# A hybrid decoder step on one core: the low weight halves of eight more phases come from adding transfers

## The chip, the cores and the metric

The kernel runs on one core of one Trainium2 chip. Its metric is the device time of one execution, in microseconds (us), given as the median of several runs; less is better. A core has a matrix engine (TensorE, in the rows PE for its matmuls and PEld for its weight loads), a vector engine (VectorE, DVE), an activation engine (ScalarE, ACT), a general engine (GpSimd, POOL) and a sequencer that mostly issues transfers (SyncE, SP). Each engine runs its own list of instructions in order; semaphores tie the lists together. Transfers are issued by SP or by GpSimd and run on 16 shared DMA engines.

## The reference

One layer of a decoder for 512 prompt tokens and 8 x 4 sample tokens (544 columns in all), in float32. The weight matrices are what is streamed; cut to them, the layer is:

```python
h = rmsnorm(x, norm1_g)
a1, a2, z, xbc, dt_raw, u, v = split(h @ w_in)
y_a = silu(layernorm(causal_dwconv(a1 * sigmoid(a2)))) @ conf_w_out
y_ssd = ssd(silu(causal_dwconv(xbc)), softplus(dt_raw + bias), ...)   # 16 heads, state 128
y_b = rmsnorm((y_ssd + D * xs) * silu(z), ssm_norm_g) @ ssm_w_out
y_c = (gelu(u) * chunk_spatial(layernorm(gelu(v)))) @ gmlp_w_out
gates = sigmoid(h @ w_gate + b_gate)                                  # three gates
x = x + (gates[0] * y_a + gates[1] * y_b + gates[2] * y_c) @ w_o
up = rmsnorm(x, norm2_g) @ ffn_w_up                                   # 2 x 2816 wide
x = x + (silu(causal_dwconv(up[..., :2816])) * up[..., 2816:]) @ ffn_w_down
```

The new states of the three convolutions, of the recurrence and the normalised v are outputs too, and y is the final rmsnorm of x.

## The kernel before

**Arithmetic.** TensorE multiplies in a rounded float32 (fp32r). For accuracy every weight and every activation is kept as a high part, which is the value rounded to fp32r, and a low part, which is the value less its high part. A product is made of three matmuls: high by high, high by low and low by high. The tokens lie in two halves of 272 columns, so one block of 128 weight rows (a k-block) costs 6 matmuls: a slot of 8 k-blocks 48, one of 6 k-blocks 36, one of 5 k-blocks 30.

**Slots, quads and phases.** `w_split[:, s, 0]` and `w_split[:, s, 1]` hold the high and low part of slot s, `w_raw[:, s]` the float32 weights as loaded. There are four slots; one filling of all four is a quad. The work is twelve phases one after the other, with their quads and the k-blocks of a slot: A (2 quads), VU (2), X (3), G2 (4), G0 (4), Z (2), G1 (4), WO (2), U1 (6), all of 8 k-blocks, where G2 and G0 have 4 in every second slot, then D1 (4 quads of 6 k-blocks), U2 (5 of 8) and D2 (4 of 5). In D1 and D2, the two parts of the last projection, two slots in a row (a pair) add up to one output block; elsewhere each slot is an output block of its own.

**The life of a slot.** SP loads the raw weights (`load_quad`, L329). When TensorE has finished the block that used the slot (`acc_full`), ACT evacuates it, then makes the slot's new parts from `w_raw` (`split_hi`, L348, called in `act_quad`, L377). In D1 and D2 the evacuation point comes once in a pair, so both slots of a pair are refilled after the pair. The low half is made in one of two ways. In the quads from the second of A to the first of Z ("added" quads, `is_added`), ACT writes the negative of the rounded weights into the low half (L352) and the high half after it (L353), and GpSimd issues a transfer that adds the raw weights from memory onto the low half (`add_raw`, L361). From the second quad of Z to the end, ACT writes only the high half, and GpSimd subtracts it from the raw weights (`split_lo`, L355, the instruction on L358). TensorE waits for the low half of a slot before the slot's first matmul (`wait_lo` in `pe_quad`, L403). In the last quad of D2 (`last_halves`, L1421) TensorE takes the first token half over all four slots and then the second half, so it comes to the second pair of slots after 30 matmuls rather than 60.

**Who waits for whom.** After its loads, SP waits for the low half of the quad before (subtracted quads) or for the high half (added quads) until it overwrites `w_raw`. GpSimd's list is in program order: `pool_phase` (L598) gives per pair the phase's own work (in the up projections the convolution's edges, L620 to L627) and then the low halves of the quad ahead. Two of its phases hold the last slot of the quad ahead until a value is ready ("hold"), and in Z (L664 to L673) the last slot of G1's first quad waits for `ssm_lo`, the split of the recurrence's output, whose room it takes. In G1 the activations come from that split, made by VectorE (L2023) out of a long chain on `xbc` (L1945, L1957, L1988).

Of the kernel before, what the change touches and what calls it, by code (L numbers as in the profile page):

```python
# [20 lines left out]
ALU = mybir.AluOpType  # L21
# [67 lines left out]
def phases():  # L89
    out, q, p = {}, 0, 0  # L90
    for name, quads, kb, per_block in PHASES:
        out[name] = Phase(name, quads, kb, per_block, q, p)
        q += quads
        p += quads * (2 // per_block)
    return out
# [19 lines left out]
def loop(e, lo, hi, body):  # L115

    if hi - lo == 1:
        body(lo)
    elif hi > lo:
        with e.Fori(lo, hi) as i:  # L120
            body(i)


def wait(e, sem, value):

    if isinstance(value, int) and value <= 0:
        return
    e.wait_ge(sem, value)
# [11 lines left out]
def build(nc, ins, outs):  # L140
    ph = phases()
    order = [x[0] for x in PHASES]
    with ExitStack() as ctx:
        def sb(name, shape, dt=F32):
            return ctx.enter_context(nc.sbuf_tensor(name, shape, dt))
# [10 lines left out]
        w_split = sb("w_split", [P, SLOTS, 2, ELEM], F32R)  # L156
# [131 lines left out]
        w_hi = [sem(f"w_hi{s}") for s in range(SLOTS)]  # L288
        w_lo = [sem(f"w_lo{s}") for s in range(SLOTS)]
        w_added = [sem(f"w_added{s}") for s in range(SLOTS)]  # L290
# [20 lines left out]
                return ins["ffn_w_up"], i * 4 + ((0 if name == "U1" else 2 * FFA) + s)  # L311
            return ins["ffn_w_down1" if name == "D1" else "ffn_w_down2"], i * 4 + s

        added_first, added_end = ph["A"].quad0 + 1, ph["Z"].quad0 + 1

        def is_added(p, i):
            return isinstance(i, int) and added_first <= p.quad0 + i < added_end

        def wait_lo(e, p, i, s, back=0):

            q = p.quad0 - back
            if isinstance(i, int) and added_first <= q + i < added_end:
                e.wait_ge(w_added[s], 16 * (q + i + 1 - added_first))
            elif isinstance(i, int) and q + i < added_first:
                wait(e, w_lo[s], q + i + 1)
            else:
                e.wait_ge(w_lo[s], i + (q + 1 - (added_end - added_first)))

        def load_quad(sp, p, i):  # L329
            for s in range(SLOTS):  # L330
                src, j = w_src(p.name, i, s)
                n = p.kb[s] * P
                if isinstance(i, int) and added_first < p.quad0 + i <= added_end:
                    sp.wait_ge(w_hi[s], i + p.quad0)
                elif not isinstance(i, int) or p.quad0 + i > 0:
                    wait_lo(sp, p, i, s, 1)
                ap = src[j] if isinstance(j, int) else src[bass.ds(j, 1)].rearrange("o p n -> (o p) n")
                sp.dma_start(w_raw[:, s, 0:n], ap).then_inc(w_landed[s], 16)

        def load_phase(sp, name, first=0):  # L340
            p = ph[name]
            if p.quad0 <= added_end:
                for i in range(first, p.quads):
                    load_quad(sp, p, i)
            else:
                loop(sp, first, p.quads, lambda i: load_quad(sp, p, i))

        def split_hi(act, p, i, s):  # L348
            n = p.kb[s] * P
# [5 lines left out]
        def split_lo(e, p, i, s):  # L355
            n = p.kb[s] * P
            e.wait_ge(w_hi[s], i + (p.quad0 + 1))
            e.tensor_tensor(w_split[:, s, 1, 0:n], w_raw[:, s, 0:n], w_split[:, s, 0, 0:n].bitcast(F32),  # L358
                               ALU.subtract).then_inc(w_lo[s], 1)

        def add_raw(pool, p, i, s):  # L361

            src, j = w_src(p.name, i, s)
            n = p.kb[s] * P
            pool.wait_ge(w_hi[s], p.quad0 + i + 1)
            pool.dma_start(w_split[:, s, 1, 0:n], src[j], accum_op=ALU.add).then_inc(w_added[s], 16)  # L366

        def head_groups():

# [227 lines left out]
        def _(pool):  # L597
            def pool_phase(name, work, hold=None):  # L598


                p = ph[name]

                def quad(i, ahead, hold=None):
                    for r in range(2):
                        work(i, r)
                        if ahead is not None:
                            split_lo(pool, ahead[0], ahead[1], 2 * r)
                            if hold is not None and r == 1:
                                pool.wait_ge(sem(hold), KD)
                            split_lo(pool, ahead[0], ahead[1], 2 * r + 1)  # L610
                loop(pool, 0, p.quads - 1, lambda i: quad(i, (p, i + 1)))
                quad(p.quads - 1, after(p), hold)

            def nothing(i, r):
# [49 lines left out]
            p = ph["Z"]  # L664
            for i in range(p.quads):
                for s in range(SLOTS):
                    q, j = (p, i + 1) if i + 1 < p.quads else after(p)
                    if (i, s) == (1, 0):
                        for n in range(STATES_Z):
                            decay_state(n)  # L670
                    if (i, s) == (1, 3):
                        pool.wait_ge(sem("ssm_lo"), KD)
                    split_lo(pool, q, j, s)  # L673
            pool_phase("G1", nothing, "mx_lo")
            pool_phase("WO", nothing, "n2_lo")
            pool.wait_ge(sem("merged"), 16)
# [1677 lines left out]
```

## Time and profile before

| what | value |
|---|---|
| runs | 1003.36, 1005.99, 1001.53 us; median 1003.36 us |
| the profiled execution | 1004.03 us; its span 1001.8 us; mean granted clock 0.996 |
| busy in the span | PE 984.0 us (98%), DVE 607.3 (61%), ACT 437.6 (44%), POOL 310.8 (31%) |
| transfers issued by GpSimd | 60 adding transfers, 27.27 MB, the queue's packets 15.5% of 16 engines |
| transfers issued by SP | 97.09 MB, 32.1% |

The profiled execution is 0.67 us above the median of the runs. A time in the rows below is counted from the start of the span. TensorE is busy nearly all the time, so what other engines do matters only where TensorE has to wait for it; the chain of waits and the timelines show such places as a number in square brackets, the idle time before a row and what ended it.

### The profile page before, as it was taken

The numbers are of one execution on the slowest core, as the hardware profiler recorded it, in microseconds if no ns is written. First come the engines' busy times: TensorE is split into PE (matmuls) and PEld (weight loads), VectorE is DVE, ScalarE is ACT, GpSimd is POOL, SyncE is SP. The second block draws the span as 40 slices with busy tenths as digits, with TensorE's granted clock in tenths as the row PEclk, the third lists the DMA queues.
The fourth block names the chain that finished last, engine by engine and source line by source line (L and its number), as shares of the span: only waits on it lengthen the run. The fifth ranks groups of instructions, "written<-read, shape, count | busy, mean of one in ns | idle before, by whom it ended". The sixth has DMA issues, their size and how long they took to land.

```text
span 1001.8 us, 19136 instructions
## 1 busy us (share of the span) xinstructions
PE 984.0 (98%) x7849; PEld 963.6 (96%) x7849; DVE 607.3 (61%) x955; ACT 437.6 (44%) x619; POOL 310.8 (31%) x261
## 2 busy tenths in 40 slices
PE   8899999999999999999999999999999999999997
PEld 8799999999998999899999999999999999999997
DVE  7599799962645675797744247555540036565456
ACT  7554579575734775525233344444321132232120
POOL 0111111111111114344342444444433464444341
PEclk9899999999999999999999999999999999999999
DMA  7888769667765768315272223222223332321222
GB/s 227 251 184 181 164 144 151 143 128 169 160 149 125 181 143 223 110 64 168 85 257 84 85 85 105 85 84 84 63 63 95 115 106 86 93 79 52 70 71 90
DMA packets 52590, 125.24 MB, mean 125 GB/s; under 512 B 15920, under 2 KB 18864, under 8 KB 52528
## 3 DMA queue, kind: packets, MB, share of 16 engines
q1 hardware_dynamic: 43744, 97.09, 32.1%
q0 software_dynamic: 8640, 27.27, 15.5%
q8 instruction: 45, 0.74, 0.3%
q14 instruction: 17, 0.14, 0.1%
q10 hardware_dynamic: 144, 0.00, 0.0%
HBM read 116.41 MB, written 7.93 MB: 124 GB/s over the span
## 4 chain that ended last, share of the span: by engine, by line
PE 90%; DVE 3%; DMA 2%; SPq 2%; ACT 1%; issue 1%; DVEq 0%; ACTq 0%
PE accs L418 82%; PE accs L1438 2%; DMA w_split<-in_w_in_main 1%; DMA w_split<-in_w_gate 1%; PE misc L1213 1%; SPq L513 1%; DVE part L494 1%; PE misc L1178 1%; DMA w_raw<-in_w_in_main 1%; PE misc L1037 1%; PE misc L1218 1%; PE misc L1197 1%; DVE xbc L1945 0%; PE misc L1163 0%; PE misc L1229 0%
## 5 line engine op out<-in xcount | busy, mean ns | idle before, releaser
L418 PE MATMUL accs<-h_split,w_split 128*128 128x272 f32 x4608 | 584.4, 288 | 0.1
L418 PEld LDWEIGHTS accs<-h_split,w_split 128*128 128x128 f32 x4608 | 576.9, 188 | 5.6 <-issue 4.4
L418 PE MATMUL accs<-branch,w_split 128*128 128x272 f32 x2472 | 320.5, 290 | 7.0 <-DMA w_split<-in_w_in_main 5.0
L418 PEld LDWEIGHTS accs<-branch,w_split 128*128 128x128 f32 x2472 | 314.3, 189 | 11.7 <-DMA w_split<-in_w_in_main 5.2
L358 POOL TENSOR_TENSOR w_split<-w_raw,w_split 128x1024 fp32r<-128x1024 f32 (+2 forms) x104 | 234.7, 2264 | 209.5 <-ACT w_split L353 186.0
L353 ACT ACTIVATE w_split<-w_raw 128x1024 fp32r<-128x1024 f32 (+3 forms) x166 | 157.8, 959 | 202.0 <-PE accs L418 201.8
L1522 DVE SCALAR_TENSOR_TENSOR ca<-part,params,ca 128x512 f32<-128x512 f32 x120 | 82.5, 744 | 0.1
L366 POOL DMA_DIRECT2D w_split<-in_w_in_main x24 | 21.1, 879 | 153.7 <-ACT w_split L353 153.7
L2202 DVE TENSOR_TENSOR xbc<-accs,xbc 128x544 f32<-128x544 f32 x14 | 10.1, 725 | 87.7 <-PE accs L418 87.7
L352 ACT ACTIVATE w_split<-w_raw 128x1024 fp32r<-128x1024 f32 (+1 forms) x60 | 56.1, 936 | 15.9 <-PE accs L418 12.7
L2179 DVE TENSOR_TENSOR temps<-temps,mixed 128x512 f32<-128x512 f32 x22 | 40.7, 1850 | 26.5 <-ACT temps L1011 26.5
L865 ACT ACTIVATE temps<-accs,params 128x544 f32<-128x544 f32 x24 | 17.2, 715 | 81.3 <-PE accs L418 81.2
L366 POOL DMA_DIRECT2D w_split<-in_w_gate x16 | 13.9, 870 | 109.8 <-ACT w_split L353 109.8
L2164 DVE TENSOR_TENSOR temps<-accs,mixed 128x272 f32<-128x272 f32 (+2 forms) x66 | 18.8, 340 | 44.0 <-PE accs L418 43.9
L2175 DVE SCALAR_TENSOR_TENSOR temps<-temps,params 128x560 f32<-128x560 f32 x44 | 37.4, 850 | 6.1 <-DVE temps L2172 1.5
L2191 DVE TENSOR_TENSOR branch<-temps,branch 128x544 f32 (+1 forms) x22 | 25.9, 1178 | 22.2 <-ACT branch L1016 22.2
L1011 ACT ACTIVATE temps<-temps,params 128x560 f32<-128x560 f32 x22 | 16.8, 764 | 47.4 <-DVE temps L2175 47.3
L1621 DVE SCALAR_TENSOR_TENSOR temps<-temps,params 128x568 f32<-128x568 f32 x36 | 29.0, 807 | 5.8 <-ACT temps L815 5.6
L2090 DVE TENSOR_TENSOR temps<-accs,temps 128x544 f32<-128x544 f32 x8 | 5.8, 725 | 37.5 <-PE accs L418 37.5
L626 POOL COPY tail_f<-temps 128x2 f32 (+1 forms) x22 | 4.5, 205 | 75.7 <-DVE temps L2164 75.7
L2144 DVE TENSOR_TENSOR xbc<-accs,xbc 128x544 f32<-128x544 f32 x8 | 5.8, 725 | 31.2 <-PE accs L418 31.2
L1908 DVE TENSOR_SCALAR temps<-misc,small 128x128 f32<-128x128 f32 x64 | 17.3, 342 | 10.6 <-PE misc L1197 10.6
(280 smaller groups left out, 793.4 us busy)
## 6 DMA issues: line engine op xcount, KB each, us to landing
w_raw<-in_ffn_w_up SPq DMA_DIRECT2D x44, 512.0 KB, 3.6
w_raw<-in_w_in_main SPq DMA_DIRECT2D x28, 512.0 KB, 4.6
w_split<-in_w_in_main POOLq DMA_DIRECT2D x24, 512.0 KB, 8.0
w_raw<-in_w_gate SPq DMA_DIRECT2D x24, 512.0 KB, 3.9
w_split<-in_w_gate POOLq DMA_DIRECT2D x16, 512.0 KB, 7.9
w_raw<-in_ffn_w_down SPq DMA_DIRECT2D x16, 384.0 KB, 3.1
w_raw<-in_ffn_w_down SPq DMA_DIRECT2D x16, 320.0 KB, 2.9
xbc<-in_x SPq DMA_DIRECT2D x16, 272.0 KB, 5.8
```

Of the source, the lines that this page charges most:

```text
L352: act.activation(w_split[:, s, 1, 0:n], w_raw[:, s, 0:n], ACT.Copy, scale=-1.0)
L353: act.activation(w_split[:, s, 0, 0:n], w_raw[:, s, 0:n], ACT.Copy).then_inc(w_hi[s], 1)
L358: e.tensor_tensor(w_split[:, s, 1, 0:n], w_raw[:, s, 0:n], w_split[:, s, 0, 0:n].bitcast(F32), ALU.subtract).then_inc(w_lo[s], 1)
L366: pool.dma_start(w_split[:, s, 1, 0:n], src[j], accum_op=ALU.add).then_inc(w_added[s], 16)
L418: mm = pe.matmul(accs[:, a, half, 0:HALF], w_split[:, s, wp, k * P:(k + 1) * P], rhs(s, k, xp, half), start=(first and k == 0 and n == 0), ...
L1438: mm = pe.matmul(accs[:, a, half, 0:HALF], w_split[:, s, wp, k * P:(k + 1) * P], rhs(s, k, xp, half), start=(s % 2 == 0 and k == 0 and n = ...
L1522: ins_ = dve.scalar_tensor_tensor(out=dst, in0=src, scalar=w, in1=dst, op0=ALU.mult, op1=ALU.add)
L1621: dve.scalar_tensor_tensor(out=cv, in0=src, scalar=w, in1=cv, op0=ALU.mult, op1=ALU.add)\
L2164: ins_ = dve.tensor_tensor(dst, src, st, ALU.mult)
L2175: dve.scalar_tensor_tensor(out=cv, in0=src, scalar=w, in1=cv, op0=ALU.mult, op1=ALU.add)\
L2179: dve.tensor_tensor(sil, sil, stat_n2[:, 0:SEQ], ALU.mult)
L2191: dve.tensor_tensor(pick(branch, i * 2 + (12 + r)), prod, pick(branch, i * 2 + r).bitcast(F32), ALU.subtract).then_inc(sem("f_lo"), 1)
```

## The change

All quads but the first of A become added ones: `is_added` holds from A's second quad to the end, also where the quad is a loop's register. ACT makes two copies for every slot, GpSimd issues an adding transfer where it subtracted, TensorE waits for that transfer's semaphore (`w_added`) and SP for ACT's (`w_hi`). `pool_phase` is written out quad by quad instead of a hardware loop, and SP's loads always run in a loop. The subtracting instructions of GpSimd that go are 72 of 128x1024, 16 of 128x768 and 16 of 128x640, and as many adding transfers come in their place. Line numbers of the changed kernel are 4 to 6 lower from L353 on.

```diff
-        added_first, added_end = ph["A"].quad0 + 1, ph["Z"].quad0 + 1
+        added_first = ph["A"].quad0 + 1
 
         def is_added(p, i):
-            return isinstance(i, int) and added_first <= p.quad0 + i < added_end
+            return not isinstance(i, int) or p.quad0 + i >= added_first
 
         def wait_lo(e, p, i, s, back=0):
 
             q = p.quad0 - back
-            if isinstance(i, int) and added_first <= q + i < added_end:
-                e.wait_ge(w_added[s], 16 * (q + i + 1 - added_first))
-            elif isinstance(i, int) and q + i < added_first:
+            if isinstance(i, int) and q + i < added_first:
                 wait(e, w_lo[s], q + i + 1)
             else:
-                e.wait_ge(w_lo[s], i + (q + 1 - (added_end - added_first)))
+                e.wait_ge(w_added[s], i * 16 + 16 * (q + 1 - added_first))
 
         def load_quad(sp, p, i):
...
-                if isinstance(i, int) and added_first < p.quad0 + i <= added_end:
+                if not isinstance(i, int) or p.quad0 + i > added_first:
                     sp.wait_ge(w_hi[s], i + p.quad0)
-                elif not isinstance(i, int) or p.quad0 + i > 0:
+                elif p.quad0 + i > 0:
                     wait_lo(sp, p, i, s, 1)
...
         def load_phase(sp, name, first=0):
             p = ph[name]
-            if p.quad0 <= added_end:
-                for i in range(first, p.quads):
-                    load_quad(sp, p, i)
-            else:
-                loop(sp, first, p.quads, lambda i: load_quad(sp, p, i))
+            loop(sp, first, p.quads, lambda i: load_quad(sp, p, i))
...
-            pool.wait_ge(w_hi[s], p.quad0 + i + 1)
-            pool.dma_start(w_split[:, s, 1, 0:n], src[j], accum_op=ALU.add).then_inc(w_added[s], 16)
+            pool.wait_ge(w_hi[s], i + (p.quad0 + 1))
+            ap = src[j] if isinstance(j, int) else src[bass.ds(j, 1)].rearrange("o p n -> (o p) n")
+            pool.dma_start(w_split[:, s, 1, 0:n], ap, accum_op=ALU.add).then_inc(w_added[s], 16)
...
                         if ahead is not None:
-                            split_lo(pool, ahead[0], ahead[1], 2 * r)
+                            add_raw(pool, ahead[0], ahead[1], 2 * r)
                             if hold is not None and r == 1:
                                 pool.wait_ge(sem(hold), KD)
-                            split_lo(pool, ahead[0], ahead[1], 2 * r + 1)
-                loop(pool, 0, p.quads - 1, lambda i: quad(i, (p, i + 1)))
+                            add_raw(pool, ahead[0], ahead[1], 2 * r + 1)
+                for i in range(p.quads - 1):
+                    quad(i, (p, i + 1))
...
                     if (i, s) == (1, 3):
                         pool.wait_ge(sem("ssm_lo"), KD)
-                    split_lo(pool, q, j, s)
+                    add_raw(pool, q, j, s)
```

GpSimd's list in D2, the last phase, before: a loop over the quads, where each row names the line, the instruction, what it writes and reads, and in brackets the semaphores it waits for.

```order
L120 UNCONDITIONAL_BRANCH
L120 ISA
L358 TENSOR_TENSOR w_split<-w_raw,w_split 128x640 [waits w_hi0]
L358 TENSOR_TENSOR w_split<-w_raw,w_split 128x640 [waits w_hi1]
L358 TENSOR_TENSOR w_split<-w_raw,w_split 128x640 [waits w_hi2]
L358 TENSOR_TENSOR w_split<-w_raw,w_split 128x640 [waits w_hi3]
L120 REGISTER_ALU
L120 COMPARE_AND_BRANCH
```

The same place after: the last two quads written out, each row a transfer from `ffn_w_down`.

```order
L361 DMA w_split<-in_ffn_w_down 128x640 [waits w_hi0]
L361 DMA w_split<-in_ffn_w_down 128x640 [waits w_hi1]
L361 DMA w_split<-in_ffn_w_down 128x640 [waits w_hi2]
L361 DMA w_split<-in_ffn_w_down 128x640 [waits w_hi3]
L361 DMA w_split<-in_ffn_w_down 128x640 [waits w_hi0]
L361 DMA w_split<-in_ffn_w_down 128x640 [waits w_hi1]
L361 DMA w_split<-in_ffn_w_down 128x640 [waits w_hi2]
L361 DMA w_split<-in_ffn_w_down 128x640 [waits w_hi3]
```

The waits are the same ones in the same order; the subtraction became a transfer's issue, and the semaphore that TensorE waits for is now counted up by the transfer's landing.

GpSimd's list at the end of Z, before: the low halves of Z's second quad, GpSimd's share of the state update (L494), and those of G1's first quad.

```order
L358 TENSOR_TENSOR w_split<-w_raw,w_split 128x1024 [waits w_hi3]
L494 TENSOR_TENSOR part<-part,small 128x512 [waits s_off,s_last]
L494 TENSOR_TENSOR part<-part,small 128x512 x3
L358 TENSOR_TENSOR w_split<-w_raw,w_split 128x1024 [waits w_hi0]
L358 TENSOR_TENSOR w_split<-w_raw,w_split 128x1024 [waits w_hi1]
L358 TENSOR_TENSOR w_split<-w_raw,w_split 128x1024 [waits w_hi2]
L358 TENSOR_TENSOR w_split<-w_raw,w_split 128x1024 [waits w_hi3,ssm_lo]
```

And after, with the same values under line numbers 5 lower.

```order
L361 DMA w_split<-in_w_in_z 128x1024 [waits w_hi3]
L489 ISA
L489 TENSOR_TENSOR part<-part,small 128x512 [waits s_off,s_last]
L489 TENSOR_TENSOR part<-part,small 128x512 x3
L361 DMA w_split<-in_w_gate 128x1024 [waits w_hi0]
L361 DMA w_split<-in_ssm_w_out 128x1024 [waits w_hi1]
L361 DMA w_split<-in_w_gate 128x1024 [waits w_hi2]
L361 DMA w_split<-in_ssm_w_out 128x1024 [waits w_hi3,ssm_lo]
```

The state update stays GpSimd's and stays at its place; before and behind it stand transfers' issues, and the last of them still waits for `ssm_lo`.

## Rows read from the trace of the kernel before

**Rows 1.** The page, first part: busy us (share of the span) x instructions.

```profile
PE 984.0 (98%) x7849; PEld 963.6 (96%) x7849; DVE 607.3 (61%) x955; ACT 437.6 (44%) x619; POOL 310.8 (31%) x261
```

**Rows 2.** The chain that ended last: start us, us, what.

```profile
599.83 375.61 PE accs L418 x3012
975.45 9.41 PE accs L1438 x75
```

**Rows 3.** Stretches: length, busy PE PEld DVE ACT POOL, clock, DMA, GB/s.

```profile
34.40:37.00 2.60, 0.00 (x0) 0.00 (x0) 1.78 (x4) 1.71 (x3) 0.00 (x0) 1.00 1.01 233
37.00:44.00 7.00, 4.62 (x20) 4.62 (x21) 5.25 (x10) 4.92 (x7) 1.83 (x2) 0.51 0.97 241
40.00:101.00 61.00, 61.00 (x476) 61.00 (x476) 54.64 (x89) 27.34 (x34) 8.89 (x11) 0.97 0.83 189
450.00:460.00 10.00, 8.39 (x63) 7.88 (x62) 7.88 (x13) 6.82 (x10) 1.74 (x1) 1.00 0.60 211
930.00:975.00 45.00, 45.00 (x361) 45.00 (x361) 20.30 (x20) 8.24 (x12) 20.37 (x11) 1.00 0.25 71
```

**Rows 4.** PE in time order, [idle before <-releaser]: 20:70 and 425:470.

```profile
39.38 26.36 PE L418 MATMUL accs<-branch,w_split 128*128 128x272 f32 x192 [4.99 <-DMA w_split<-in_w_in_main]
...
430.60 0.94 PE L1364 MATMUL misc<-branch 96*128 96x512 f32 x3
...
437.35 1.46 PE L1364 MATMUL misc<-branch 96*128 96x512 f32 x3
...
455.86 2.70 PE L418 MATMUL accs<-branch,w_split 128*128 128x272 f32 x18 [1.60 <-DVE branch L2023]
...
466.05 4.17 PE L418 MATMUL accs<-branch,w_split 128*128 128x272 f32 x32
```

**Rows 5.** DVE in order of time, 425 to 460 us.

```profile
431.87 2.88 DVE L1945 TENSOR_TENSOR xbc<-xbc,temps 128x512 f32<-128x512 f32 x1
...
443.42 0.69 DVE L1945 TENSOR_TENSOR xbc<-xbc,temps 128x512 f32<-128x512 f32 x1
```

**Rows 6.** POOL in order of time, 423 to 470 us.

```profile
428.58 5.62 POOL L358 TENSOR_TENSOR w_split<-w_raw,w_split 128x1024 fp32r<-128x1024 f32 x2
...
458.26 4.74 POOL L358 TENSOR_TENSOR w_split<-w_raw,w_split 128x1024 fp32r<-128x1024 f32 x2 [16.68 <-DVE branch L2023]
```

**Rows 7.** Line L366, the adding transfers: issue ns, landing us; then windows 185:204, 229:232.

```profile
L366 POOL DMA_DIRECT2D w_split<-in_w_in_main x24: 853/868/1016, 30.2 to 175.6; - x24
...
DMA to landing us min/median/max: 4.4/7.8/12.6
...
DMA to landing us min/median/max: 4.4/4.7/8.1
...
DMA to landing us min/median/max: 8.5/8.6/8.7
```

**Rows 8.** POOL's and ACT's groups by form: busy us, mean ns, idle before.

```profile
L358 POOL TENSOR_TENSOR w_split<-w_raw,w_split 128x1024 fp32r<-128x1024 f32 x72 | 176.3, 2451 | 140.9 <-ACT w_split L353 117.3 <-DVE branch L2023 16.7 <-DVE branch L2106 6.8
...
L353 ACT ACTIVATE w_split<-w_raw 128x1024 fp32r<-128x1024 f32 x118 | 123.9, 1052 | 102.2 <-PE accs L418 102.0
```

**Rows 9.** PE in order of time, 735 to 1002 us.

```profile
738.56 72.32 PE L418 MATMUL accs<-branch,w_split 128*128 128x272 f32 x576
...
930.19 45.26 PE L418 MATMUL accs<-branch,w_split 128*128 128x272 f32 x360
975.29 9.57 PE L1438 MATMUL accs<-branch,w_split 128*128 128x272 f32 x75
```

**Rows 10.** ACT in order of time, in D1 and D2.

```profile
747.87 1.58 ACT L353 ACTIVATE w_split<-w_raw 128x768 fp32r<-128x768 f32 x2 [7.31 <-PE accs L418]
...
937.99 1.37 ACT L353 ACTIVATE w_split<-w_raw 128x640 fp32r<-128x640 f32 x2 [5.70 <-PE accs L418]
...
975.48 1.37 ACT L353 ACTIVATE w_split<-w_raw 128x640 fp32r<-128x640 f32 x2 [6.06 <-PE accs L418]
```

**Rows 11.** POOL in order of time, D2's end.

```profile
976.30 3.58 POOL L358 TENSOR_TENSOR w_split<-w_raw,w_split 128x640 fp32r<-128x640 f32 x2 [3.35 <-ACT w_split L353]
```

## The prediction

> **What bounds the kernel now.** I read the engines' busy time first: TensorE works 984.0 of 1001.8 us [rows 1], so all its idle time is 17.8 us and no change to the other engines can gain more than that. The chain of waits says where it is: from 599.83 us on, the chain is 3012 matmuls without a break for 375.61 us, then the last quad [rows 2]; one matmul is 375.61 / 3012 = 0.1247 us. So from the first up projection to the last quad nothing is to be gained, and everything that comes late is paid in full. What can be gained lies before, and of it the change touches only the end of Z, where the timeline of TensorE shows two stalls on VectorE: 1.60 us before 455.86, and three small products that take 1.46 us where their like take 0.94, about 0.5 us [rows 4]. The rows on the adding transfers give the new operation's price: 0.86 us of GpSimd to issue one, and 4.4 to 12.6 us until it has landed, 7.8 in the middle [rows 7]. A subtraction takes 2.45 us for 128x1024 [rows 8] and 1.8 for 128x640 (two in 3.58) [rows 11]. The low half of a slot thus comes some 4 to 6 us later than now wherever GpSimd is not backed up, and the question at each slot is whether TensorE is then still busy with the others.
>
> **Where the delay is hidden.** With one block a slot, a refilled slot is needed again after the three other slots, 3 x 48 x 0.1247 = 18.0 us. Evacuation and two copies take some 4 us, a landing 7.8, so 6 us remain in U1, U2, WO and G1, and I cost these at nothing; without that cover each landing above 14 us would be paid. ACT's second copy, 72 x 1.05 us and 32 of 0.7 to 0.8, brings it from 438 to about 537 us of 1002 [rows 1, 8]: hidden, as ACT's wait for TensorE before these copies is 102 us. SP gets its go from ACT's high half instead of from GpSimd, so raw loads start earlier; they were landed in time already: nothing. GpSimd's unrolled list: nothing, since it is busy 31% [rows 1] and loses 235 us of subtractions for 104 x 0.87 = 90 us of issues. The extra traffic is 104 adds, about 47 MB over the last 550 us; the DMA engines are 0.25 busy there now [rows 3].
>
> **The end of Z (a gain).** The first VectorE row at 431.87 takes 2.88 us while GpSimd subtracts from 428.58 on, and its like at 443.42, with GpSimd at rest, 0.69 [rows 5, 6]. VectorE has no pause from there to the split that ends the 1.60 us stall. Without the subtractions the chain comes 2.2 us earlier, which covers 1.60 and 0.5: -2.1. Bounds: -2.1 (nothing else is there to gain) and 0 (if the issues of transfers hold VectorE up the same way). Against it stands the hold on slot 3 of G1's first quad: what GpSimd waited 16.68 us for came at 458.26 [rows 6]; 2.2 earlier is 456.06, and with a landing of 7.8 it is there at 463.9. TensorE starts on that slot at 466.05 [rows 4], 2.1 earlier 463.95. That is level, so I add 0.3 for scatter; a landing of 12.6 would cost 4.7.
>
> **Into U2 (a loss).** In D1 both slots of a pair are refilled after the pair and needed again after one other pair. A pair of D1 takes 72.32 / 8 = 9.04 us [rows 9]. ACT starts 0.27 us after the end of it (747.87 less 738.56 and 9.04) [rows 9, 10]; two copies of U2's 512 KB slot take 2.10 [rows 8]; GpSimd starts 0.13 after a copy (976.30 less 975.48 and one copy of 0.69) [rows 10, 11]. Left for the landing: 9.04 - 0.27 - 2.10 - 0.13 = 6.5 us. Two adds close together landed after 8.5 to 8.7 us (the last line of [rows 7]); I take 8.6: late by +2.1, once, at U2's first slot. Bounds 0 and 6.1 (a landing of 12.6).
>
> **Within D1.** The same with copies of 1.58: 7.06 us are left for 384 KB. The stretch with two 256 KB adds and one of 512 KB, each alone, has 4.4, 4.7 and 8.1 [rows 7]; on a line from 4.4 to 8.1, 384 KB take 6.25, and a partner cost 8.7 - 8.1 = 0.6: 6.85. Just in time; +0.2 for scatter, bounds 0 and 4.6 (three late pairs at 8.6).
>
> **Within D2.** A pair takes 45.26 / 6 = 7.54 us [rows 9], ACT starts 0.26 after it and makes two copies in 1.37 [rows 10]: 7.54 - 0.26 - 1.37 - 0.13 = 5.78 us are left. By the same line 320 KB take 5.3, with a partner 5.9: late by 0.1. A late pair gives the next one as much more room, so only the first pair of each of three quads pays: +0.3. In the last quad the second pair is needed after 30 matmuls, 3.74 us. ACT starts at 975.48, 0.19 after the pair before has ended [rows 9, 10], so 3.74 - 0.19 - 1.37 - 0.13 = 2.05 us are left where a subtraction needs 1.8 today. It is late by 5.9 - 2.05 - 0.1 = +3.75. D2 together +4.1; bounds +2.3 (the least landing of the trace, 4.4) and +12 (8.6 for every pair).
>
> **The clock.** After the one long wait on an add, 4.99 us, the next 192 matmuls took 26.36 us instead of 23.94 [rows 4]; the granted clock was 0.51 (1.2 of 2.4 GHz) from 37 to 44 us after 1.00 before it. After the 1.60 us stall it stayed at 1.00 [rows 3]. The 3.75 us wait in the last quad lies nearer to the first: +2.4, bounds 0 and 2.4.
>
> **Sum.** -2.1 + 0.3 + 2.1 + 0.2 + 4.1 + 2.4 = +7.0, that is 1011.0 for the profiled execution of 1004.03, which lies 0.67 above the median; on the median of 1003.36 it is 1010.4.
>
> A rule that would change the sum: the Trainium skill, "DMA: Bandwidth & Descriptors", section "Anatomy of one DMA — SWDGE (gpsimd) path", fits a transfer issued by GpSimd as 2.0 us plus its bytes over 436 GB/s, by which 320 KB would be an estimated 2.75 us and 512 KB 3.2. Only the last quad would then be late, by 0.7, and the sum would be -1.1, 1002.3. The trace disagrees for the adding form: none of 60 landed in under 4.4 us [rows 7]; what the rule would do is part of rival (3) below.
>
> **Rivals.** (1) All as above, but the clock holds through the 3.75 us wait: +4.6, 1008.0. For it: the only drop in the rows came after 5 us with the DMA full. (2) The adds land quicker where little else is moved: in D2 the DMA engines are 0.25 busy against 0.83 from 40 to 101 us, in the stretch of the earlier adds [rows 3]. With 5.1 us for 320 KB (midway from 4.4 to 5.9) and 7.8 for the 512 KB pair: D2 +3.05, U2 +1.3, gain -2.1, sum +2.2, 1005.6; with the clock's drop 1008.0. (3) Not slower: adds so quick that only the last quad waits. From 4.1 us for 320 KB on down, and 6.5 for 512 KB, its wait is paid by the gain at Z; at 4.4, the least of the 60, the sum is +0.3, 1003.7. Against it: that least one moved 256 KB. (4) GpSimd's issues suffer from VectorE, so that an add takes 8.6 us even in D2: three pairs late by 2.8, the last one by 3.75, D1 +4.6, U2 +2.1, clock +2.4, gain -2.1: +19.2, 1022.6. Against it: issues took 853 to 1016 ns over the whole trace, where VectorE was busy 54.64 of 61 us too, and the middle landing was 7.8 [rows 3, 7]. The skill's "SBUF — State Buffer", section "SBUF: two separate sides", warns of just this, that some VectorE instructions keep GpSimd from writing a transfer's descriptors; that busy stretch does not bear it out. (5) VectorE is not freed, or slot 3 of G1 is caught by its hold: the gain is lost and up to 1.7 us come on top, +9 to +11, 1012.4 to 1014.
>
> **How the numbers follow.** The case of the sum 0.42, (1) 0.15, (2) 0.20, (3) 0.06, (4) 0.06, (5) 0.11. A measurement of this kernel tells 0.5%, 5.0 us, from no change; the border is 1008.4. The case of the sum lies 2 us above it and counts 0.85 slower (0.36); (1) lies on it, 0.45 (0.07); (2) 0.25 (0.05); (4) all (0.06); (5) 0.8 (0.09): slower 0.63. Faster than 998.3 needs more than the 2.1 us I can find: 0.04. Same: 0.33. The likeliest's own range is 1007 to 1014; the range takes in (2) down to 1004.5 and (5) and half of the way to (4) up to 1016. Predicted: 1010.4.
>
> **What the profile of the changed kernel would show.** The adds of 320 KB with their landing times: 5.3 to 6.5 us bears the D2 step out, under 4.5 kills it. TensorE's timeline: a wait on the add of `ffn_w_down` of 3 to 4.5 us within the last quad, one of 1 to 3 us at U2's first slot, almost none inside U1, U2, WO and G1, and no 1.6 us stall on VectorE at the end of Z. The granted clock behind the last wait: 0.5, or 1.0 for rival (1). VectorE's row at the place of 431.87 at 0.7 instead of 2.88. Waits above 2 us at every pair of D2 would be rival (4). The prediction is wrong if waits show up in the one-block phases, where I count on 6 us of room.

## The result and the profile after

The changed kernel takes 1010.73 us (median of 7 runs, 1008.74 to 1012.23) against 1003.51 us (7 runs, 1001.53 to 1005.99): ratio 1.0066, interval 1.0053 to 1.0079. It is slower by 0.66%, some 6.6 us (the two medians are 7.2 us apart), and the forecast was 1010.4. The spans of the two profiled executions, 1008.5 and 1001.8 us, differ by 6.7. The total fits, but most of its larger terms don't, in both directions, as the stretches show. (The title counts eight more phases; there are seven: the second quad of Z, G1, WO, U1, D1, U2 and D2.) Each number is the time from a phase's first weight matmul to the next phase's, taken from the starts in TensorE's timelines; the last quad of D2 stands with all that follows it.

| stretch | before | after | difference | forecast |
|---|---|---|---|---|
| up to the end of A | 65.57 | 64.37 | -1.20 | 0 |
| VU, X, G2, G0 | 316.67 | 316.33 | -0.34 | 0 |
| Z and G1 | 163.63 | 160.98 | -2.65 | -1.8 |
| WO and U1 | 192.69 | 192.71 | 0.0 | 0 |
| D1, with the wait for U2's first slot | 72.16 | 75.19 | +3.03 | +2.3 |
| U2 | 119.47 | 119.56 | +0.1 | 0 |
| D2, three quads | 45.10 | 48.49 | +3.39 | +0.3 |
| the last quad and the rest | 26.54 | 30.90 | +4.36 | +6.2 |

The list of what TensorE waited for, summed by line (us in all, times, the longest), shows the places at once:

```profile
PE accs L413 <- DMA w_split<-in_ffn_w_down: 4.3, 6, 1.3
PE accs L413 <- DMA w_split<-in_w_in_main: 4.0, 1, 4.0
PE accs L1434 <- DMA w_split<-in_ffn_w_down: 2.5, 1, 2.5
...
PE accs L413 <- DMA w_split<-in_ffn_w_up: 0.4, 1, 0.4
```

The first, third and fourth are new: adds into the slots of D1, D2 and of U2's first quad, of which there were none before. TensorE's timeline shows them one by one, in the place of the unbroken stretches of [rows 9]:

```profile
762.40 18.30 PE L413 MATMUL accs<-branch,w_split 128*128 128x272 f32 x144 [0.80 <-DMA w_split<-in_ffn_w_down]
780.97 9.29 PE L413 MATMUL accs<-branch,w_split 128*128 128x272 f32 x72 [0.26 <-DMA w_split<-in_ffn_w_down]
790.86 18.30 PE L413 MATMUL accs<-branch,w_split 128*128 128x272 f32 x144 [0.60 <-DMA w_split<-in_ffn_w_down]
809.58 119.73 PE L413 MATMUL accs<-h_split,w_split 128*128 128x272 f32 x960 [0.42 <-DMA w_split<-in_ffn_w_up]
929.14 22.71 PE L413 MATMUL accs<-branch,w_split 128*128 128x272 f32 x180
953.15 7.78 PE L413 MATMUL accs<-branch,w_split 128*128 128x272 f32 x60 [1.30 <-DMA w_split<-in_ffn_w_down]
961.46 7.77 PE L413 MATMUL accs<-branch,w_split 128*128 128x272 f32 x60 [0.52 <-DMA w_split<-in_ffn_w_down]
970.01 7.79 PE L413 MATMUL accs<-branch,w_split 128*128 128x272 f32 x60 [0.78 <-DMA w_split<-in_ffn_w_down]
977.63 3.94 PE L1434 MATMUL accs<-branch,w_split 128*128 128x272 f32 x30
984.12 7.46 PE L1434 MATMUL accs<-branch,w_split 128*128 128x272 f32 x45 [2.54 <-DMA w_split<-in_ffn_w_down]
```

A wait costs some 0.3 us more than its bracket: from 929.14 to 977.63 are 48.49 us, 3.39 more than before, and the three brackets make 2.60. The last 45 matmuls took 7.46 us, where 45 at 0.1247 make 5.6. The stretches before, behind and further behind that wait (length, busy PE, PEld, DVE, ACT, POOL, then the granted clock, the share of the DMA engines, GB/s) say why, and the last two rows, cut finer, show that the clock was at its half level until about 988.5 us and full in the 3 us behind:

```profile
975.00:984.00 9.00, 6.58 (x53) 6.36 (x51) 3.50 (x6) 4.11 (x6) 1.74 (x2) 1.00 0.51 75
984.10:987.00 2.90, 2.88 (x16) 2.88 (x17) 0.00 (x0) 0.00 (x0) 0.00 (x0) 0.68 0.47 86
987.00:992.00 5.00, 5.00 (x37) 5.00 (x37) 1.32 (x3) 0.00 (x0) 0.00 (x0) 0.85 0.00 0
...
985.20:988.40 3.20, 3.20 (x16) 3.20 (x15) 0.00 (x0) 0.00 (x0) 0.00 (x0) 0.50 0.09 16
988.60:991.60 3.00, 3.00 (x27) 3.00 (x25) 1.32 (x3) 0.00 (x0) 0.00 (x0) 1.00 0.00 0
```

The landing times of the adds (least, middle, most) in D1 from 753 to 786 us, in D2 from 940 to 966, and of the last pair from 979 on:

```profile
DMA to landing us min/median/max: 7.3/7.8/8.6
...
DMA to landing us min/median/max: 6.5/7.3/8.0
...
DMA to landing us min/median/max: 4.5/5.0/5.4
```

The same 320 KB take 7.3 us in the middle of D2 and 4.5 to 5.4 at its end, where no raw load of a next quad is left. The adds that TensorE waited for, as the chain that ended last has them (issue, us to landing):

```profile
754.57 7.80 DMA w_split<-in_ffn_w_down
...
802.55 6.91 DMA w_split<-in_ffn_w_up
...
946.10 7.01 DMA w_split<-in_ffn_w_down
...
962.70 7.27 DMA w_split<-in_ffn_w_down
...
979.56 4.52 DMA w_split<-in_ffn_w_down
```

Not every pair is that slow. The first add of D2's first pair, issued at 938.68 us beside two raw loads and its partner like the later ones, landed in 4.6 us, and that of D1's first pair (at 745.64) in 5.7; neither made TensorE wait. What sets such pairs apart stays open: two kernels below with the same D2 up to its last quad have first adds of 4.2, 5.7, 7.0 and 7.2 us (g3_warm) and of 7.2, 4.8, 7.1 and 6.5 us (h3_warm10).

The DMA engines, 0.25 busy in D2 before [rows 3], are 0.67 busy there now:

```profile
929.00:975.00 46.00, 43.40 (x342) 42.76 (x341) 11.72 (x18) 15.02 (x23) 9.58 (x11) 1.00 0.67 143
```

And the gain at Z. Two rows of VectorE before, besides those of [rows 5]:

```profile
424.80 7.15 DVE L494 TENSOR_TENSOR part<-part,small 128x512 f32<-128x512 f32 x4
...
439.46 3.33 DVE L2005 SCALAR_TENSOR_TENSOR xbc<-xbc,params,temps 128x32 f32<-128x32 f32 x8
```

VectorE's and TensorE's rows now, which answer to these and to [rows 4, 5]:

```profile
423.25 4.97 DVE L489 TENSOR_TENSOR part<-part,small 128x512 f32<-128x512 f32 x4
428.20 0.69 DVE L1941 TENSOR_TENSOR xbc<-xbc,temps 128x512 f32<-128x512 f32 x1
...
433.61 1.39 DVE L2001 SCALAR_TENSOR_TENSOR xbc<-xbc,params,temps 128x32 f32<-128x32 f32 x8
...
448.51 1.47 DVE L2019 SCALAR_TENSOR_TENSOR branch<-xbc,params,branch 128x544 fp32r<-128x544 f32 x2
```

```profile
435.80 0.88 PE L1360 MATMUL misc<-branch 96*128 96x512 f32 x3
...
448.95 5.42 PE L413 MATMUL accs<-branch,w_split 128*128 128x272 f32 x42
```

The row that took 2.88 us takes 0.69, the ones of 7.15 and 3.33 us take 4.97 and 1.39, and the 24 and 18 matmuls between which the 1.60 us stall lay are one row of 42.

### The profile page after: what moved, and what is told of

Its sections match the earlier page's. It is cut to its first block, busy times and chain, and to the rows that moved or that the text cites. A ratio compares the mean times of both kernels' runs of the same rounds, so it can differ in the third digit from the quotient of the medians.

```text
span 1008.5 us, 19250 instructions
## 1 busy us (share of the span) xinstructions
PE 985.7 (98%) x7849; PEld 964.6 (96%) x7849; DVE 529.8 (53%) x955; ACT 524.9 (52%) x723; POOL 164.7 (16%) x261
## 3 DMA queue, kind: packets, MB, share of 16 engines
q0 software_dynamic: 23616, 76.56, 43.1%
## 4 chain that ended last, share of the span: by engine, by line
PE 90%; DMA 5%; SPq 2%; ACT 1%; issue 1%; DVE 0%; DVEq 0%; ACTq 0%
PE accs L413 81%; DMA w_split<-in_ffn_w_down 3%; PE accs L1434 1%; PE misc L1209 1%; SPq L508 1%; DMA w_split<-in_w_in_main 1%; DMA w_split<-in_ffn_w_up 1%; PE misc L1174 1%; ACT w_split L347 1%; DMA w_raw<-in_w_in_main 1%; PE misc L1033 1%; PE misc L1214 1%; PE misc L1193 1%; PE misc L1159 0%; PE misc L1225 0%
## 5 line engine op out<-in xcount | busy, mean ns | idle before, releaser
L346 ACT ACTIVATE w_split<-w_raw 128x1024 fp32r<-128x1024 f32 (+3 forms) x164 | 157.3, 959 | 203.7 <-PE accs L413 199.9
L347 ACT ACTIVATE w_split<-w_raw 128x1024 fp32r<-128x1024 f32 (+3 forms) x166 | 157.9, 952 | 0.0
L1518 DVE SCALAR_TENSOR_TENSOR ca<-part,params,ca 128x512 f32<-128x512 f32 x120 | 82.4, 741 | 0.1
L2198 DVE TENSOR_TENSOR xbc<-accs,xbc 128x544 f32<-128x544 f32 x14 | 10.1, 724 | 101.6 <-PE accs L413 101.6
L361 POOL DMA_DIRECT2D w_split<-in_ffn_w_up x44 | 38.3, 870 | 103.2 <-ACT w_split L347 101.4
L361 POOL DMA_DIRECT2D w_split<-in_w_gate x24 | 20.8, 869 | 148.5 <-ACT w_split L347 148.5
L361 POOL DMA_DIRECT2D w_split<-in_ffn_w_down x32 | 27.8, 870 | 103.6 <-ACT w_split L347 103.4
L2171 DVE SCALAR_TENSOR_TENSOR temps<-temps,params 128x560 f32<-128x560 f32 x44 | 35.3, 801 | 6.1 <-DVE temps L2168 1.5
L2187 DVE TENSOR_TENSOR branch<-temps,branch 128x544 f32 (+1 forms) x22 | 16.0, 725 | 35.5 <-ACT branch L1012 35.5
L2175 DVE TENSOR_TENSOR temps<-temps,mixed 128x512 f32<-128x512 f32 x22 | 15.2, 693 | 26.5 <-ACT temps L1007 26.5
L2184 DVE TENSOR_TENSOR temps<-accs,temps 128x272 f32<-128x272 f32 (+2 forms) x66 | 18.8, 340 | 13.6 <-PE accs L413 13.5
```

The costliest lines, as they stand in the source:

```text
L346: act.activation(w_split[:, s, 1, 0:n], w_raw[:, s, 0:n], ACT.Copy, scale=-1.0)
L347: act.activation(w_split[:, s, 0, 0:n], w_raw[:, s, 0:n], ACT.Copy).then_inc(w_hi[s], 1)
L361: pool.dma_start(w_split[:, s, 1, 0:n], ap, accum_op=ALU.add).then_inc(w_added[s], 16)
L1518: ins_ = dve.scalar_tensor_tensor(out=dst, in0=src, scalar=w, in1=dst, op0=ALU.mult, op1=ALU.add)
L2171: dve.scalar_tensor_tensor(out=cv, in0=src, scalar=w, in1=cv, op0=ALU.mult, op1=ALU.add)\
L2184: ins_ = dve.tensor_tensor(dst, src, sil, ALU.mult)
```

## The experiments

Two theories stood for D1 and D2: R, the raw loads slow the adds, because SP now starts them at the same moment (it waits for ACT where it waited for GpSimd's subtraction); P, the two adds of a pair slow each other. The edits are against the changed kernel unless said otherwise.

**e1_raw_later**: raw loads after the adds.

```diff
+                if p.name in ("D1", "U2", "D2"):
+                    wait_lo(sp, p, i, s, 1)
-                if not isinstance(i, int) or p.quad0 + i > added_first:
+                elif not isinstance(i, int) or p.quad0 + i > added_first:
                     sp.wait_ge(w_hi[s], i + p.quad0)
```

> The changed kernel, but in D1, U2 and D2 the raw load of a slot's next weights waits until the slot's add has landed, instead of only until ACT has read the raw weights. Theory R (the raw loads, which in the changed kernel start at the same moment as the add, slow the adds of a pair): the first add of a pair in D2 lands in 4.2 to 5.0 us, as in the last two pairs where no raw load is left, instead of 7.0 to 7.6; the pair waits of D1 and D2 (3.0 and 3.4 us longer than before) go nearly, the wait in the last quad (2.54 us) stays; 1005 us, about 5.5 less than the changed kernel. Rival P (the two adds of a pair slow each other): landings stay at 7 to 7.6 us, time within 1 us of the changed kernel.

Measured: 1004.95 us, ratio to before 1.002 (1.000 to 1.004). D1 took 72.70 us instead of 75.19. In the middle of D2 (942 to 964 us) the adds landed in

```profile
DMA to landing us min/median/max: 4.7/5.2/6.0
```

and no pair waited; R holds. But three quads of D2 took 46.97 us, not 45.1, because the last quad's first slot waited, and the wait at its third shrank:

```profile
972.46 4.05 PE L1436 MATMUL accs<-branch,w_split 128*128 128x272 f32 x30 [1.72 <-DMA w_split<-in_ffn_w_down]
976.79 6.14 PE L1436 MATMUL accs<-branch,w_split 128*128 128x272 f32 x45 [0.28 <-DMA w_split<-in_ffn_w_down]
```

The add for that first slot was issued at 965.09 and took 7.33 us; SP issued the store of the convolution's tails at 965.30. i1_store_early below takes that up.

**e2_adds_apart**: one add of a pair after the other.

```diff
+                            if name in ("D1", "D2"):
+                                wait_lo(pool, ahead[0], ahead[1], 2 * r)
                             add_raw(pool, ahead[0], ahead[1], 2 * r + 1)
```

> The changed kernel, but while D1 and D2 run GpSimd issues the second add of each pair only when the first has landed; raw loads as in the changed kernel. Rival P (the two adds slow each other): the first add lands in 4.5 to 5.5 us, the first slot of a pair is in time, the second, needed 3.7 or 4.5 us later, is just late by up to 1; 1007 to 1009 us. Theory R (raw loads slow the adds): the first add still takes 6.5 us or more, the second lands 12 us or more after the first's issue and TensorE waits 2 to 4 us for it at each of 12 pairs: 1025 us or more.

Measured: 1016.65 us, ratio 1.0154 (1.0113 to 1.0194), between the two forecasts. In D2 the first adds landed in 5.6 to 5.8 us, the second ones, alone, in 4.2 to 4.4:

```profile
DMA to landing us min/median/max: 4.2/5.6/5.8
```

So P has its part as well. The first pair of D2 left out, a first add of 320 KB takes 5.6 to 5.8 us beside raw loads alone, here, and 7.0 to 7.6 beside raw loads and its partner, in the changed kernel; with its partner alone, in the last quad, it takes 4.2 to 4.5. Neither by itself makes a first slot late (5.78 us are left); together they did so at three of the four pairs. D2's three quads took 47.53 us instead of 48.49, but more than that was lost at the second slots: D1 took 76.22 us instead of 75.19 and the last stretch 33.46 instead of 30.90, since in the last quad the adds now queued up three times:

```profile
981.95 2.16 PE L1436 MATMUL accs<-branch,w_split 128*128 128x272 f32 x15 [1.23 <-DMA w_split<-in_ffn_w_down]
985.07 2.16 PE L1436 MATMUL accs<-branch,w_split 128*128 128x272 f32 x15 [0.97 <-DMA w_split<-in_ffn_w_down]
989.80 5.38 PE L1436 MATMUL accs<-branch,w_split 128*128 128x272 f32 x30 [2.57 <-DMA w_split<-in_ffn_w_down]
```

**e3_sub_down**, and again as **e3_again**: subtraction in D1 and D2.

```diff
         def is_added(p, i):
-            return not isinstance(i, int) or p.quad0 + i >= added_first
+            return p.name not in ("D1", "D2") and (not isinstance(i, int) or p.quad0 + i >= added_first)
```

(and the counts that follow from it).

> The changed kernel with the low halves of D1 and D2 alone made by GpSimd's subtraction again (one copy of ACT there), adds everywhere else. If the loss is D1 and D2 and the last quad (in the trace 2.3 + 3.4 + 4.4 us, with 0.8 at U2's first slot left) and the end of Z a gain of 2.6 us: 1000.5 to 1001.5 us, faster than the kernel before by 0.2 to 0.3%. If the adds of the one-block phases cost something that the timeline doesn't show, or the gain at Z were chance: 1003.5 or more.

Measured: 1003.77 us, ratio 1.0007 (0.9987 to 1.0027).

> The same kernel as e3_sub_down once more (subtraction in D1 and D2, adds elsewhere), beside the next one on the same chip. By the stretches of its trace it should be 2 us below the kernel before, 1001.5 us; the first time it was only 0.4 below. If that was chance: 1001 to 1002; if not: 1003.5 again.

Measured: 1002.76 us, ratio 0.999 (0.9977 to 1.0002). The loss is gone both times, and D2 and the last quad stand at 45.10 and 26.53 us as before the change; Z and G1 keep 160.98. But the times stay 1 to 3 us above the forecasts. Part of it is U2's first slot, whose 512 KB add still lands late by 0.3 (D1 72.47 and 72.45 us), more in the next run; the rest lies in stretches that differ from run to run (A 58.8 and 59.6, G2 82.4 and 80.8 us) and is not settled.

**g4_unrolled**: e3 with SP's early loads written out as in the kernel before.

```diff
+            if p.quad0 <= ph["Z"].quad0 + 1:
+                for i in range(first, p.quads):
+                    load_quad(sp, p, i)
+                return
```

> e3_sub_down with SP's loads of VU, X, G2, G0 and Z written out as in the kernel before, instead of in hardware loops. If the loops cost what e3_sub_down missed: 1.5 to 2 us below e3_again. If they cost nothing: equal to it within 1 us.

Measured: 1004.59 us, ratio 1.0009 (0.9995 to 1.0023), 1.8 us above e3_again, not below. The loops are not the cause; in this trace U2's first slot was late by 1.6 us (D1 73.78).

**e5_z_only**, against the kernel before: adds for the eight slots at the end of Z. With them the raw loads of G1's first two quads wait for ACT's high half instead of GpSimd's subtraction.

```diff
-        added_first, added_end = ph["A"].quad0 + 1, ph["Z"].quad0 + 1
+        added_first, added_end = ph["A"].quad0 + 1, ph["G1"].quad0 + 1
...
-                    split_lo(pool, q, j, s)
+                    add_raw(pool, q, j, s)
```

> The kernel before with adds only up to the first quad of G1, so that only the eight subtractions of the end of Z are gone. Theory (the gain is VectorE freed from GpSimd's subtractions there): the 1.60 us stall at 455.86 and the 0.5 us one at 437 are gone, 2.6 us less than the kernel before, 1000.9 us. Rival (the gain comes from elsewhere, the loops or the first phases): the stalls stay and the time is within 1 us of the kernel before.

Measured: 1001.79 us, ratio 0.998 (0.9962 to 0.9999); Z and G1 160.98 us instead of 163.63. The whole gain at Z and G1 comes from taking out these eight subtractions; the other stretches that got shorter in the changed kernel, A and G2, are taken up below.

**g3_warm** and **h3_warm10**: small matmuls in the last wait.

```diff
                         if half == 0:
+                            if s == 2:
+                                keep_warm(20)      # 10 in h3_warm10
                             wait_lo(pe, p, i, s)
```

> The changed kernel with 20 more small matmuls into an unused corner of PSUM (about 2.2 us at 0.11 us each) in the last quad, between the second slot and the wait for the third, so that TensorE is hardly idle there. Theory (the clock falls because TensorE stood idle for 2.5 us): the granted clock stays at 1.00 behind the wait and the 45 matmuls of the last quad after it take 5.9 us instead of 7.46; 1.5 us less in the last stretch, about 1009 us. Rival (the clock would fall there anyway, or the small matmuls count as nothing): still 7 us or more, no gain.

Measured: 1012.36 us, ratio 1.0103 (1.0065 to 1.0141); no gain, since 20 of them took 4.63 us, not 2.2 (each of them is two of the 40 counted here, and 0.11 us is what one of the two takes). But the clock:

```profile
980.62 4.63 PE L1049 MATMUL misc<-consts 128*128 128x128 f32 x40
985.00 5.89 PE L1436 MATMUL accs<-branch,w_split 128*128 128x272 f32 x45
```

```profile
984.00:987.00 3.00, 3.00 (x28) 3.00 (x27) 0.00 (x0) 0.00 (x0) 0.00 (x0) 1.00 0.24 44
```

The same 45 matmuls take 5.89 us instead of 7.46: it is TensorE standing idle that lowers the clock there, and the price is 1.6 us. The length of such a wait doesn't settle it alone. These are the 192 matmuls behind the wait for the first add of A's second quad, in e1_raw_later and in i1_store_early (the next experiment; up to there both are the changed kernel):

```profile
37.53 25.85 PE L415 MATMUL accs<-branch,w_split 128*128 128x272 f32 x192 [2.58 <-DMA w_split<-in_w_in_main]
```

```profile
36.91 24.33 PE L415 MATMUL accs<-branch,w_split 128*128 128x272 f32 x192 [2.63 <-DMA w_split<-in_w_in_main]
```

Behind the first the granted clock was 0.50 from 38.6 to 41.8 us, behind the second it stayed at 1.00.

> As g3_warm, but with 10 small matmuls, 2.3 us by what 20 took there (4.6 us): less than the wait of 2.5 us. If idleness sets the clock: granted clock 1.00 behind the wait, the last stretch (from the last quad's first matmul to the end) 29.2 us instead of 30.9. Rival: a rest of idleness is enough to lower the clock, 30.5 us or more.

Measured: one run, 1010.53 us; clock 1.00, last stretch 29.74 us instead of 30.90, where 29.2 was forecast. The last two adds landed 6.29 and 8.70 us after the quad's first matmul, much as in the changed kernel (6.45 and 8.69); waits of 0.16 and 0.26 us remain behind the small matmuls, and 1.2 of the 1.6 us came back.

**i1_store_early**: e1 with the tails' store moved.

```diff
-            for name in ("WO", "U1", "D1", "U2", "D2"):
+            for name in ("WO", "U1", "D1", "U2"):
                 load_phase(sp, name)
+            load_quad(sp, ph["D2"], 0)
             sp.wait_ge(sem("tail_f"), 2 * NF)
             sp.dma_start(outs["conv_ffn"], tail_f[:, :, :]).then_inc(sem("stored_tails"), 16)
+            load_phase(sp, "D2", first=1)
```

> e1_raw_later with the store of the convolution's tails (198 KB) issued between the raw loads of D2's first and second quad, instead of behind the last raw load. There it was issued at 965.30 us, 0.2 us after the add that then took 7.33 us. If the store slowed that add: the add lands in 4.3 to 5.5 us, the 1.72 us wait at the last quad's first slot goes, the wait at its third slot grows from 0.28 to about 2 us, since nothing moves it any more, and with it the granted clock may fall: D2's three quads 45.1 us, the last stretch 28.7 to 30.5. If not: the add still takes 7 us.

Measured: one run, 1003.11 us. The add landed in 4.95 us, D2's three quads took 45.10 us, and the last stretch 30.82, a little above the forecast's 30.5, with the old wait and the old clock (0.72 from 977 to 983 us):

```profile
976.48 7.44 PE L1438 MATMUL accs<-branch,w_split 128*128 128x272 f32 x45 [2.50 <-DMA w_split<-in_ffn_w_down]
```

So, by this one execution, the store was it, and the last quad's wait doesn't depend on raw loads: there it is the short room of 2.05 us against a landing of 4.5.

**g1_vu_later**, and again as **g1_again**: what R says of the rest of the kernel. Against e5_z_only, which is the kernel before with the gain at Z:

```diff
+                if p.name == "VU":
+                    wait_lo(sp, p, i, s, 1)
-                if isinstance(i, int) and added_first < p.quad0 + i <= added_end:
+                elif isinstance(i, int) and added_first < p.quad0 + i <= added_end:
                     sp.wait_ge(w_hi[s], i + p.quad0)
```

> e5_z_only (adds up to G1's first quad) with the raw loads of both quads of VU held until the add into the same slot has landed. By what e1_raw_later showed in D2, the first add of A's second quad, which lands in 6.8 to 9.3 us beside raw loads and makes TensorE wait 2.6 to 5.7 us, should land in 5 to 6.5 us: 2 to 4 us less than e5_z_only, 998 to 1000 us. Rival (the transfers of the start, not VU's raw loads, slow that add, or VU's own raw weights then come late): no gain, or a loss at VU's first slots.

Measured: 997.47 us, ratio to before 0.9937 (0.9919 to 0.9955), half a us below the forecast's range. The first add of A's second quad landed in 5.4 us, and the wait of 4.99 us with the half clock behind it [rows 4] became

```profile
35.87 24.32 PE L420 MATMUL accs<-branch,w_split 128*128 128x272 f32 x192 [1.23 <-DMA w_split<-in_w_in_main]
```

where 192 matmuls take 24.32 us, not 26.36.

> g1_vu_later once more, beside h1_all_later on one chip: 997 to 998 us, 0.6% under the kernel before.

Measured: 997.77 us, ratio 0.9931 (0.9917 to 0.9945). The add landed in 6.0 us here, and TensorE waited 2.23. In the eleven traces of kernels that don't hold VU's raw loads this wait was 2.6 to 5.7 us and the landing 6.8 to 9.3; in the three that do (h1_all_later below is the third) the wait was 1.2 to 2.2 and the landing 5.4 to 6.0. This is the fastest version of all runs.

**h1_all_later**: adds everywhere but in the very last quad, raw loads of VU, D1, U2 and D2 after the adds.

```diff
+            return added_first <= p.quad0 + i < ph["D2"].quad0 + 3
...
+                if before_added and p.name not in ("VU", "D1", "U2", "D2"):
                     sp.wait_ge(w_hi[s], i + p.quad0)
```

> Adds for every quad but the very last of D2 (which GpSimd subtracts), and raw loads of VU, D1, U2 and D2 held until the add into the same slot has landed. If raw loads beside the adds and the short room of the last quad are the whole loss: D1 72.2 to 72.7 us, the three other quads of D2 45.1, the last stretch 26.5, A 53; 997 to 998.5 us, level with g1_again. If adds have another price in D1 and D2: 1000 or more.

Measured: 1000.32 us, ratio 0.9955 (0.9944 to 0.9967). That is on the side of the second forecast. But in the trace D2 and the last stretch are at 45.10 and 26.54 us, as with subtraction, and of the places that the change touched only U2's first slot still waits:

```profile
804.58 119.74 PE L432 MATMUL accs<-h_split,w_split 128*128 128x272 f32 x960 [0.85 <-DMA w_split<-in_ffn_w_up]
```

So by this trace adds in D1 and in D2 before its last quad cost nothing but that slot (1.0 us here), and yet bring nothing over subtraction. The rest of the 2.5 us to g1_again is not settled: the execution traced was the fastest of six, and its span, 995.8 us, is level with g1_again's 996.1.

## Why the prediction was right, and where its terms were not

**The direction and the bound.** TensorE had nothing to win behind 600 us and lost at the three places named: U2's first slot, the pairs of D1 and D2, the last quad. The one-block phases hid the landings, as costed: WO and U1 192.71 us against 192.69, U2 119.56 against 119.47.

**The gain at Z** was right in its mechanism, and e5 shows it by itself: -2.65 us instead of -2.1. The difference is what a stall costs beyond its bracket: the 1.60 us one cost 2.06 (G1 took 100.77 us before and 98.71 after), the other 0.59 (Z, 62.86 and 62.27). The hold on G1's slot 3, costed at 0.3, didn't bind: the split that had ended the stall started 6.5 us earlier (448.51 against 455.02), 5.0 without the 1.5 that A and G2 had brought, not 2.2. The prediction counted one row of the chain as slowed by GpSimd's subtractions (2.88 us); the two of 7.15 and 3.33 us were so too (2.2, 2.2 and 1.9 us; a pause of 1.3 us behind them took part of that back). The add into slot 3 was issued at 452.10 us, right behind the end of the hold, and TensorE started on the slot at 461.86 without a wait.

**The step that failed** is a sentence of the second part: "raw loads start earlier; they were landed in time already: nothing". They were in time, but from then on they ran beside the adds, and e1 shows what that costs. The 0.25 by which the DMA engines were counted as busy was the load without the adds; with them it is 0.67 in D2. (The new adds move 76.56 less 27.27 MB, which is 49.3 and not 47.) The landing of a first add in D2, put at 5.9 us by a line through adds of other phases, was 7.0 to 7.6 at the three pairs that waited, and that of D1, put at 6.85, 7.3 to 8.0 at all but the first pair. The terms of D1 and D2 therefore came out as +2.3 (D1 without U2's first slot) and +3.4 us instead of +0.2 and +0.3.

**Two terms were too large.** U2's first slot: an add of 6.91 us instead of 8.6, so 0.8 us instead of 2.1. The last quad: no raw load is left there, the add landed in 4.5 us, and the wait cost 2.75 us (984.12 less 977.63 and 3.74) instead of 3.75; the clock's drop was there, at 1.6 us instead of 2.4. It fell to the same half level, but for less of the work. After the 4.99 us wait of the kernel before, it was at that level for the first 4.4 us of the work:

```profile
39.40:43.80 4.40, 4.40 (x19) 4.40 (x20) 2.88 (x5) 2.52 (x5) 0.96 (x1) 0.50 0.92 238
44.00:48.00 4.00, 4.00 (x34) 4.00 (x33) 0.27 (x1) 0.00 (x0) 0.00 (x0) 1.00 1.05 267
```

Here it was so for little more than the 3.2 us of the row shown with the result. And some 0.4 us of the 2.4 were not the clock's: at the full clock the 192 matmuls take 24.32 us in g1_vu_later, not 23.94.

**The sum** of the terms in the trace is -2.65 + 3.03 + 0.09 + 3.39 + 4.36 = +8.2; the other 1.5 us to the span's +6.7 lie in A and G2, where the change moves nothing but the form of SP's loads, and where the traces of kernels that don't touch VU's loads differ among themselves (A 54.6 to 60.4 us). That the forecast of +7.0 was met so closely was luck in part: errors of both signs met.

**The rivals.** The clock did not hold through the last wait, (1), and VectorE was freed, against (5). The last quad was not the only place that waited, against (3). Quick adds, (2), were half right: quick they are, 4.2 to 4.5 us for a first add in the last quad, where no raw loads are left, but not beside raw loads. GpSimd's issues held up by VectorE, (4): VectorE worked 3.59 of 9 us from 945 to 954 while an add took 7.01, and the adds became quick with the raw loads later and VectorE's work the same; so this did not happen. The rule of the Trainium skill that was weighed ("DMA: Bandwidth & Descriptors", "Anatomy of one DMA — SWDGE (gpsimd) path", 2.75 us for 320 KB) stays refuted for the adding form by these traces: no add of 320 KB landed in under 4.2 us, alone or not, and the quickest of all, one of 256 KB in h1_all_later, took 4.07.

## What to carry to other kernels

When a semaphore is replaced, ask for every queue that waited on it, the prefetch's too: a load that starts earlier is not free if it runs beside a transfer that something waits for. Hold prefetches until the urgent transfer has landed, where they have a full round to spare. Compare a landing with the room of the tightest slot (here pairs, 5.8 us, and a quad taken in another order, 2.05 us), not with the average.

## What the runs showed of the hardware

Together, neighbours can cost a transfer more than the sum of what each costs it alone: an adding transfer of 320 KB landed after 4.2 to 4.4 us alone (the second adds of e2), 4.2 to 4.5 with a partner, 5.6 to 5.8 beside raw loads, 7.0 to 7.6 beside both, at the pairs that waited. The raw loads suffer too: from 940 to 966 us of the changed kernel, and from 942 to 964 of e1, their landings were

```profile
DMA to landing us min/median/max: 3.1/5.1/6.7
```

```profile
DMA to landing us min/median/max: 2.8/3.1/4.5
```

VectorE was held up by GpSimd's subtractions far beyond Z: the group of its sums in the up projections took 1850 ns each on average before (first row) and 693 now (second row),

```profile
L2179 DVE TENSOR_TENSOR temps<-temps,mixed 128x512 f32<-128x512 f32 x22 | 40.7, 1850 | 26.5 <-ACT temps L1011 26.5
...
L2175 DVE TENSOR_TENSOR temps<-temps,mixed 128x512 f32<-128x512 f32 x22 | 15.2, 693 | 26.5 <-ACT temps L1007 26.5
```

and VectorE's busy time fell from 607.3 to 529.8 us, all of it off the path but for Z. The Trainium skill, "SBUF — State Buffer", section "SBUF: two separate sides", says that a VectorE instruction with two inputs in SBUF and a GpSimd one that reads SBUF keep each other out for a whole instruction; 1850 against 693 ns agrees.
